# Contiguous 8 KB expert pieces, slot weights in parts, and down pieces by column halves in a one-core mixture-of-experts block

## The reference

```python
h = modulate(rms_norm(x, norm_ffn_g), shift, scale)      # 256 x 1024
scores = sigmoid(h @ router_w)                           # 16 experts, a group of 4 is picked, the top 2 in it
for e in range(16):
    he = silu(h @ w_gate[e]) * (h @ w_up[e])             # 1024 -> 512
    out = out + combine[:, e:e + 1] * (he @ w_down[e])   # 512 -> 1024
x = x + gate_ffn * out
return rms_norm(x, final_norm_g)
```

## Time and profile before

| | us |
|---|---|
| median of three runs | 624.14 |
| the profiled execution | 625.4 |
| its span, first to last instruction | 623.5 |
| TensorE busy | 579.7 (93%) |
| VectorE busy | 316.7 (51%) |
| ScalarE busy | 229.3 (37%) |

### The profile page before, as it was taken

How to read it: one execution, slowest core, us unless ns; L and a number is a source line. 1 busy time by engine, 2 the same in 40 slices (tenths; PEclk the granted TensorE clock), 3 DMA queues, 4 the chain that set the end, 5 groups by cost and what they waited for, 6 DMA issues and landing times.

```text
span 623.5 us, 8315 instructions
## 1 busy us (share of the span) xinstructions
PE 579.7 (93%) x3522; PEld 428.6 (69%) x3522; DVE 316.7 (51%) x467; ACT 229.3 (37%) x312; POOL 5.7 (1%) x14
## 2 busy tenths in 40 slices
PE   1599999999999999999999999989999999999784
PEld 0499988999998888999999885534543533533232
DVE  3797976767569786786464754312202122220203
ACT  4425748444555365376543434201201111110103
POOL 3000000000000000000000000000000000000000
PEclk9799999999999999999999998999999999999997
DMA  8996553785857944744599897399999999999981
GB/s 316 362 387 227 203 203 130 276 290 219 300 216 284 399 155 162 270 139 165 174 387 357 320 383 268 114 398 389 399 387 400 387 402 387 402 387 401 387 350 69
DMA packets 80584, 184.77 MB, mean 296 GB/s; under 512 B 5561, under 2 KB 5665, under 8 KB 78497
## 3 DMA queue, kind: packets, MB, share of 16 engines
q1 hardware_dynamic: 78018, 184.06, 79.6%
q10 hardware_dynamic: 2528, 0.16, 0.3%
HBM read 183.16 MB, written 1.05 MB: 295 GB/s over the span
## 4 chain that ended last, share of the span: by engine, by line
PE 82%; DMA 9%; DVE 4%; ACT 2%; SPq 2%; issue 1%; DVEq 0%; ACTq 0%
PE ps L1357 29%; PE ps L1365 15%; PE ps L1568 15%; PE ps L1580 7%; DMA ring<-in_w_down_e_dram 3%; DMA ring<-in_w_gate_e_dram 2%; DMA ring<-in_w_up_e_dram 2%; DMA raw<-in_w_in_dram 2%; PE ps L1604 2%; PE ps L1556 2%; PE ps L1345 1%; SPq L444 1%; PE ps L1523 1%; PE ps L1434 1%; PE ps L1470 1%
## 5 line engine op out<-in xcount | busy, mean ns | idle before, releaser
L803 DVE TENSOR_TENSOR lo<-raw,hi 128x2048 fp32r<-128x2048 f32 x52 | 118.8, 2291 | 43.3 <-ACT hi L539 43.0
L1357 PE MATMUL ps<-u_hi,hi 128*128 128x256 f32 x432 | 124.4, 288 | 1.1 <-DVE u_lo L869 1.1
L1357 PE MATMUL ps<-u_lo,hi 128*128 128x256 f32 x432 | 122.2, 283 | 0.0
L1357 PE MATMUL ps<-u_hi,lo 128*128 128x256 f32 x432 | 122.2, 283 | 0.0
L1568 PE MATMUL ps<-ring,xe_t 128*64 128x512 f32 x512 | 113.8, 594 | 7.6 <-DMA ring<-in_w_up_e_dram 3.9
L539 ACT CAST hi<-raw 128x2048 fp32r<-128x2048 f32 x52 | 98.7, 1906 | 51.4 <-PE ps L1357 24.6
L1568 PEld LDWEIGHTS ps<-ring,xe_t 128*64 128x64 f32 x512 | 37.5, 137 | 75.3 <-issue 75.2
L1357 PEld LDWEIGHTS ps<-u_hi,hi 128*128 128x128 f32 x432 | 82.8, 192 | 1.5 <-DVE u_lo L869 1.3
L1357 PEld LDWEIGHTS ps<-u_lo,hi 128*128 128x128 f32 x432 | 82.8, 192 | 0.2
L1357 PEld LDWEIGHTS ps<-u_hi,lo 128*128 128x128 f32 x432 | 82.8, 192 | 0.0
L1580 PE MATMUL ps<-ring,he_t 128*64 128x512 f32 x256 | 57.1, 596 | 1.5 <-DMA ring<-in_w_down_e_dram 0.7
(11 more groups left out here) (297 smaller groups left out, 803.3 us busy)
## 6 DMA issues: line engine op xcount, KB each, us to landing
raw<-in_w_in_dram SPq DMA_DIRECT2D x42, 1024.0 KB, 5.0
ring<-in_w_gate_e_dram SPq DMA_DIRECT2D x32, 1024.0 KB, 14.6
ring<-in_w_up_e_dram SPq DMA_DIRECT2D x32, 1024.0 KB, 14.2
ring<-in_w_down_e_dram SPq DMA_DIRECT2D x32, 1024.0 KB, 14.4
raw<-in_ada_w_dram SPq DMA_DIRECT2D x16, 1024.0 KB, 5.0
first_ada<-in_ada_w_dram SPq DMA_DIRECT2D x16, 512.0 KB, 11.6
raw<-in_w_branch_m_dram SPq DMA_DIRECT2D x4, 1024.0 KB, 7.2
raw<-in_w_out_dram SPq DMA_DIRECT2D x4, 1024.0 KB, 6.3
```

What stands on the lines that cost most here:

```text
L803: V.tensor_tensor(lo[b % RING][:], src[:], hi[b % RING][:].bitcast(F32), ALU.subtract).then_inc(lo_ready, 1)
L1357: ins = mm(dst, w[:, k, cols], x[:, k0 + k, :], start=(first and c % 2 == 0 and k == 0 and n == 0), stop=(end and k == KB - 1 and n == 2), ...
```

## The change

Pieces: a piece of w_gate or w_up is now rows h * 512 + 4p + k, k = 0 to 3, in partition p, so that one partition reads 8 KB from one place; a piece of w_down is rows h * 256 + 2p + k, k = 0 and 1, also 8 KB. The other operand must lie in the same order. So x_res is read at a step of four words where it is transposed and where `xg_hi` and `xg_lo` are made (`near`, `nearby`, `dealt`), the router's weights and the norm's gain are loaded in that order, the two rows of `mod` are copied in that order to `mod_p` by ScalarE before TensorE turns them, and `he` is transposed at a step of two words.

Slot weights: VectorE splits them once into high and low fp32r parts (`weights`), the matmul has four columns in place of two and both operands in fp32r, and `w_slot` is the sum of two columns.

Last pieces: the last four pieces (w_down of experts 14 and 15) are loaded by column halves: first all rows of the left 512 columns, in two DMAs an expert, then the right columns, in two DMAs an expert with a semaphore for the second. TensorE finishes the left half (`last_down(0, ...)`) before the right.

End: y's left half is gated, rounded and split after the left half of down, and scattered before the right half is ready; four dummy matmuls follow. The root's table is loaded ahead of the last rounding; the squares of both left halves come before those of the right; the left results are multiplied by the gain on VectorE early and scaled by ScalarE at the end, the right ones are made on VectorE.

```diff
             def load(slot, p, part, e):
                 matrix, half = PARTS[part]
-                w = matrices[matrix][(2 * p + e) % NE].rearrange("(k p) n -> p k n", p=P)
-                k = w.shape[1] // 2
-                sp.dma_start(ring[slot][:].rearrange("p (k n) -> p k n", k=k), w[:, half * k:(half + 1) * k, :]
-                             ).then_inc(ring_loaded[slot], 16)
+                w = matrices[matrix][(2 * p + e) % NE].rearrange("(h p k) n -> p h (k n)", h=2, p=P)
+                sp.dma_start(ring[slot][:], w[:, half, :]).then_inc(ring_loaded[slot], 16)
...
+            def load_columns(slot, e, h, q_of, done):
+
+                w = matrices["down"][NE - 2 + e].rearrange("(h p k) n -> p h k n", h=2, p=P)
+                for q in q_of:
+                    sp.dma_start(ring[slot][:].rearrange("p (k n) -> p k n", k=KB)[:, 2 * q:2 * q + 2, :],
+                                 w[:, q, :, h * NB:(h + 1) * NB]).then_inc(done, 16)
+
+            for e in range(2):
+                n = CHUNKS - 4 + e
+                sp.wait_ge(chunk_used, n - RSLOTS + 1)
+                load_columns(n % RSLOTS, e, 0, (0, 1), ring_loaded[n % RSLOTS])
+            for q in range(2):
+                for e in range(2):
+                    n = CHUNKS - 2 + e
+                    sp.wait_ge(chunk_used, n - RSLOTS + 1)
+                    load_columns(n % RSLOTS, e, 1, (q,), last_loaded[e] if q else ring_loaded[n % RSLOTS])
...
-            act.dma_start(rows[96:104, :], A["norm_ffn_g"][0].rearrange("(c p) -> c p", p=P)).then_inc(rows_loaded, 16)
+            act.dma_start(ffn_g[:], A["norm_ffn_g"][0].rearrange("(h p k) -> p h k", h=2, p=P)).then_inc(rows_loaded, 16)
...
+                if s == M_TURN_AT[1]:
+
+                    after(act, "a_score3")
+                    act.wait_ge(ada_done, ADA_FIRST + ADA_REST)
+                    for m in range(2):
+                        ins = nc.scalar.copy(dealt(mod_p[:, m, :]), nearby(mod[:, 1 + m, :]))
+                    event(ins, "mod_p")
...
-                event(A_(xg_hi[:, t, :], x_res[:, t, :], ACT.Copy, scale=st[:, 14 + t:15 + t]), f"xg_hi{t}")
+                event(A_(dealt(xg_hi[:, t, :]), nearby(x_res[:, t, :]), ACT.Copy, scale=st[:, 14 + t:15 + t]), f"xg_hi{t}")
...
+            def last_norm():
+
+                for n in range(2 * TT):
+                    if n:
+                        act.wait_ge(squared, n)
+                    last_square(n % TT, n // TT)
+                    if n >= TT:
+                        t = n - TT
+                        act.wait_ge(last_var, t + 1)
+                        A_(st[:, 32 + t:33 + t], st[:, 20 + t:21 + t], ACT.Sqrt).then_inc(last_sqrt, 1)
+                for t in range(TT):
+                    act.wait_ge(last_rms, t + 1)
+                    A_(result[:, t, 0:NB], result[:, t, 0:NB], ACT.Copy, scale=st[:, 34 + t:35 + t]).then_inc(out_act, 1)
...
-                V.scalar_tensor_tensor(out=xg_lo[:, t, :], in0=x_res[:, t, :], scalar=st[:, 14 + t:15 + t],
-                                       in1=xg_hi[:, t, :].bitcast(F32), op0=ALU.mult, op1=ALU.subtract).then_inc(xg_split, 1)
+                for h in range(2):
+                    view = (slice(None), t, slice(h * NB, (h + 1) * NB))
+                    ins = V.scalar_tensor_tensor(out=dealt(xg_lo[view]), in0=nearby(x_res[view]), scalar=st[:, 14 + t:15 + t],
+                                                 in1=dealt(xg_hi[view].bitcast(F32)), op0=ALU.mult, op1=ALU.subtract)
+                ins.then_inc(xg_split, 1)
+            split_weights(weights, comb_tab[:, :, 0:NE], 1).then_inc(weights_split, 1)
...
-                    ins = mm(ps[7][:, T:T + 2], onehot[:, t, col:col + 2 * SLOTS].bitcast(F32), weights[:, t, :],
+                    ins = mm(ps[7][:, T:T + 4], onehot[:, t, col:col + 2 * SLOTS], pair[:, t].rearrange("p e w -> p (e w)"),
                              start=(t == 0), stop=(t == TT - 1))
...
-                    ins = tr(ps[6][:, k * P:(k + 1) * P], he[:, k * P:(k + 1) * P], ident[:])
+                    ins = tr(ps[6][:, k * P:(k + 1) * P], he[:, near(0, k, 2)], ident[:])
...
+                    slots = [(2 * (p * NPART + 4) + e) % RSLOTS for e in range(2)]
+                    for e in range(2):
+                        pe.wait_ge(ring_loaded[slots[e]], 16 * ((CHUNKS - 4 + e) // RSLOTS + 2))
+                    last_down(0, range(KB), slots)
+                    slots = group_slots(p * NPART + 5)
+                    last_down(1, (0, 1), slots)
+                    for e in range(2):
+                        pe.wait_ge(last_loaded[e], 16)
+                    last_down(1, (2, 3), slots)
...
+                if h == 0:
+                    for _ in range(4):
+                        mm(ps[4][:], scat[1][:, 0:P], y_hi_e[:, 0:NB], start=True, stop=True)
```

More of the change, by code:

```diff
@@ L109, with near, nearby, dealt @@
 CHUNKS = 2 * PAIRS * 6
+def near(start, kk, k):
+    return slice(start + kk // k * k * P + kk % k, start + (kk // k + 1) * k * P, k)
+def nearby(row):
+    return row.rearrange("q (h p k) -> q h k p", p=P, k=KB)
+def dealt(row):
+    return row.rearrange("q (h k p) -> q h k p", p=P, k=KB)
 PARTS = [(matrix, half) for matrix in ("gate", "up", "down") for half in range(2)]
@@ L189, in build @@
         scat = [at("scat0", 174, [P, T], F32R), at("scat1", 175, [P, T], F32R)]
+        mod_p = at("mod_p", 120, [P, 2, D])
         result = at("result", 120, [P, TT, D])
@@ L315, in plan @@
                 if s == M_TURN_AT[1]:
-                    act.append("ha_hi"); dve.append("ha_lo")
+                    act += ["ha_hi", "mod_p"]; dve.append("ha_lo")
                 if s == FFN_COL_AT[1]:
@@ L775, in _ @@
                 round_y(VISITS * PAIRS - 1)
+                last_norm()
             with act.If(again == 0):
+                A_(st[:, 31:32], st[:, 2:3], ACT.Sqrt)
                 round_y(PAIRS - 1)
[L779 to L789 removed]
+                last_norm()
         @block.vector
@@ L1186, in fill_xe, with gate_y @@
                 ins.then_inc(xe_dve, 1)
-            def gate_y():
-                for h in range(2):
+            def gate_y(halves=(0, 1)):
+                for h in halves:
                     ins = V.tensor_tensor(y_e[:, h * NB:(h + 1) * NB], ps[6 + h][:], mod[:, 3, h * NB:(h + 1) * NB], ALU.mult)
@@ L1203, in take_slots @@
                     rows_s = slice(64 * s, 64 * s + 64)
-                    ins = V.tensor_copy(w_slot[rows_s, side:side + 1], ps[7][rows_s, T + s:T + s + 1])
+                    ins = V.tensor_reduce(w_slot[rows_s, side:side + 1], ps[7][rows_s, T + 2 * s:T + 2 * s + 2], AX_X, ALU.add)
                 ins.then_inc(scat_ready, 1)
@@ L1485, in _ @@
                 if s in FFN_COL_AT:
-                    pe.wait_ge(ada_done, ADA_FIRST + ADA_REST)
-                    after(pe, "a_turned3")
+                    after(pe, "mod_p", "a_turned3")
                     m = FFN_COL_AT.index(s)
                     for k in range(KT):
-                        ins = mm(ps[6][:, KT * m + k:KT * m + k + 1], mod[:, 1 + m, k * P:(k + 1) * P], ones[:, 0:1],
+                        ins = mm(ps[6][:, KT * m + k:KT * m + k + 1], mod_p[:, m, k * P:(k + 1) * P], ones[:, 0:1],
                                  start=True, stop=True)
@@ L1583, in down, with last_down, turn_slots @@
                                 ins.then_inc(chunk_used, 1)
-            def turn_slots(col, weights):
+            def last_down(h, kk_of, slots):
+                for kk in kk_of:
+                    for s in range(2):
+                        w = ring[slots[s]][:].rearrange("p (k n) -> p k n", k=KB)
+                        ins = mm(ps[6 + h][64 * s:64 * s + 64, :], he_t[:, kk, s * SLOTS:(s + 1) * SLOTS], w[:, kk, :],
+                                 start=(kk == 0), stop=(kk == KB - 1))
+                        if kk == KB - 1:
+                            ins.then_inc(chunk_used, 1)
+            def turn_slots(col, pair):
                 for t in range(TT):
@@ L1660, in _ @@
                 pe.wait_ge(he_t_ready, p + 1)
-                for half in range(2):
-                    down(half, group_slots(p * NPART + 4 + half))
+                if p < PAIRS - 1:
+                    for half in range(2):
+                        down(half, group_slots(p * NPART + 4 + half))
+                else:
+                    slots = [(2 * (p * NPART + 4) + e) % RSLOTS for e in range(2)]
[7 more added lines that the diff above has]
+                    last_down(1, (2, 3), slots)
             after(pe, "many")
```

92 lines of the change are left out of this document (48 added, 44 removed).

## The result

The changed kernel took **616.39 us** (median of 5, 615.92 to 619.51) against 624.14 for the kernel before (622.63 to 625.43, 5): a ratio of 0.9885, 95% interval 0.9858 to 0.9913. Forecast were 613.4 and a range of 609.8 to 618.5; against the kernel before that is a gain of 10.7 us forecast and of 7.8 measured. The profiled execution took 615.92 us, of which 614.0 are the span.

A forecast was written before the change was run, and what follows sets the result against it. Late expert weights set the end; without them (-9.5 us) TensorE binds. Last down at 602.8 plus a 9.7 tail gives a 612.5 span, 614.4 for the profiled execution, 613.4 us median; range 609.8 to 618.5 (8 in 10).

The forecast's parts named there:

- The bound and the 8 KB rows: Expert stage: weights come late; 8 KB rows at 416 GB/s end that, -9.5 us, leaving TensorE the bound.
- The rival that memory sets the limit: Expert weight stream: DMAs do not speed up with longer rows, 621.2 us; chance 0.09.
- the one of places that collide: Expert weight stream: engines' reads meet in one part of memory; at 365 GB/s the run takes 637 us; chance 0.05.
- TensorE's path: TensorE's work up to the last down matmul: 601.65 - 1.2 + 1.5 + 0.3 + 0.5 = 602.8 us.
- Slot weights -1.2: Slot-weight matmuls: two fp32r records replace four fp32 ones, -1.2 us over eight pairs (bounds -0.9 to -1.4).
- xg_lo +1.5: VectorE before the second gather: four stepped instructions replace two, +1.5 us (bounds +0.2 to +2.5).
- mod_p +0.3: ScalarE's two copies before TensorE turns mod_p: mostly covered, +0.3 us (0 to 1.5).
- Transposes of x_res +0.5: TensorE's 16 transposes of x_res read at a step of four words: +0.5 us.
- Transposes of he 0: TensorE's transposes of he at a step of two words, eight times four: no cost.
- Rival (b): Stepped reads double he's transposes, eight times 0.49, path +3.9: 617.3 us; chance 0.22 together with (a).
- The tail: From the last down to the end: column halves and reordered end take 9.7 us against 12.4, -2.7 (-2 to -3.3).
- (a): 8 KB rows run at 407, stream stays the bound, xg_lo costs its upper bound: 616.6 us; chance 0.22 with (b).

The follow-up runs named there:

- Experiment 7: Changed kernel with the right half of each token tile stored before the left: 619.23 us.
- experiments 5 and 6: Changed kernel with the last four down pieces whole, tail dummies kept: 621.04 us; changed kernel without the four tail dummies: 619.37 us.
- experiments 6 to 9: Changed kernel, singly: no tail dummies 619.37 us; right half stored first 619.23; dummies before the mod_p wait 619.27; dummies before the x_res transpose waits 619.23.
- changed, 1st and 2nd: The changed kernel with no further edit, measured twice: 616.39 us, then 616.9 us as a yardstick.
- mod_p filled: Changed kernel with four plain fp32 dummy matmuls ahead of TensorE's wait for mod_p: 619.27 us.
- x_res filled: Changed kernel with three dummy matmuls ahead of each of TensorE's two waits for the x_res transposes: 619.23 us.
- all filled: Changed kernel with dummies in TensorE's idle stretches between 310 and 425 us, second tile's start sums moved, right half stored first: 619.24 us.
- filled once: Edits of the all filled kernel, but one dummy at each of three places and eight after xg_hi in place of ten: 614.98 us.
- experiment 2: Changed kernel with ring pieces loaded in 4 KB rows, two DMAs of 512 KB a piece: 622.14 us.

## Why the prediction was right, step by step

**The bound and the 8 KB rows: right.** 421 GB/s against 416 (and 418 by the second way), no wait for the ring, last landing about 597.2 against 596.8, pair periods to 0.1 us. The single ada block of the earlier trace rows was a good witness, and the fixed cost in a row, which I had worked out as 8.4 ns, is 9.2. The rival that memory sets the limit falls, and so does the one of places that collide. The Trainium skill (DMA: Bandwidth & Descriptors, Where 436 GB/s comes from) has the memory side at some 358 GB/s a core and the fabric at 435. The 421 measured here over 130 us, with one core at work, are above the first, so it did not bind here, and below the second.

**TensorE's path: forecast 602.8 for the end of the last down, measured 603.33.** The terms, with what the profile gives for each:
- Slot weights -1.2: -1.8 (0.22 a pair, below the lower bound).
- xg_lo +1.5: +1.8, the mean of four being 1.12 us, where VectorE's adjacent ones take 0.74. (The 3.2 that the prediction set beside its term uses a row of the Trainium skill, Vector Engine (DVE) Microarchitecture Reference, section 5.2, for both sources or the destination stepping. Here one source steps, and 3.2 did not come.)
- mod_p +0.3: +0.9. The two copies took 4.1 us in place of my 3.3; ScalarE pays a step of four words with 2.1 us against 1.05 (the adjacent cast to y_hi, L735, of the same size; least, median and most in ns):
```profile
L723 ACT COPY mod_p<-mod x2: 2099/2122/2144, 312.3 to 314.3; 128x1024 f32<-128x1024 f32 x2
```
```profile
L735 ACT CAST y_hi<-sig_gm x2: 1047/1049/1051, 349.3 to 357.0; 128x1024 fp32r<-128x1024 f32 x2
```
- Transposes of x_res +0.5: some +0.15.
- Transposes of he 0: **+0.8**, 0.1 in each of eight pairs. The prediction counted x_res alone and put he at nothing. The matmuls' records are about as long as before (283 ns against 273); the loads of the stationary operand, which read he, are half as long again:
```profile
L1671 PEld LDWEIGHTS ps<-ident,he x32: 195/209/219, 413.8 to 594.9; 128*128 128x128 f32 x32
L1671 PE MATMUL ps<-ident,he x32: 281/283/388, 413.8 to 595.1; 128*128 128x128 f32 x32
```
The same load in the kernel before:
```profile
L1597 PEld LDWEIGHTS ps<-ident,he x32: 138/140/144, 411.3 to 602.3; 128*128 128x128 f32 x32
```
In pair 2 the second of the four matmuls starts 0.22 us after the first, where it was 0.17, and the others follow at 120 ns in place of 109: together the 0.1. That the load sets this pace is my reading of it and was not tried by itself. The Trainium skill (Advanced Engine Details and Errata, SBUF Cachelines) says that two hits in 16 bytes absorb the latency. The trace does not agree: he has two, and the load takes 209 ns in place of 140. Rival (b) had the direction, at a fifth of its price, and the prediction's sign of being wrong, transposes of he above 0.5 us for four, did come, with 0.60.
- Together these miss by 0.75. The clock gives back 0.2: the fall at 319 cost 1.5 (block 43 took 7.35 us in place of 5.86), and the one that the kernel before has at 381 was absent in this execution (start sums 3.5 in place of 5.2). 0.75 - 0.2 is the 0.5 measured. That the sum came so near is in part luck: five terms missed by 0.3 to 0.8 each, with both signs, and two falls of the clock, which it did not have, cancel.

**The tail: forecast 9.7, measured 10.7.** Up to the last result it took 6.7 us, forecast 6.8. From there I let the end follow after 2.45 us, as before, and a second store issue of 0.4. It followed after 3.95 (610.05 to 614.0), because all four stores queue behind the wait for ScalarE's half. Experiment 7 gives 0.8 of this back. The sum had no order of waits in it; that is the term that was mis-sized, 2.85 for 3.95. The clock in it was right, but not for its reason: the dummies are not what kept it at 1.00 (experiments 5 and 6).

**The median.** The span was 614.0 against 612.5. The other half of the miss is my step from the profiled execution to the median: I took off 1.26 us because that of the kernel before lay above its median, while that of the changed kernel lay 0.47 below its own. (By the text's own numbers that step gives 613.1; I wrote 613.4.) The measured 616.39 lies in the stretch from 615.5 to 620 that the prediction gave to (a) and (b), though neither happened: the rate was 421, and he cost 0.8, not 3.9. The 3.0 us between forecast and median are 1.0 of tail, 0.5 of path and 1.5 of the step from one execution to the median. What goes with the spread of the executions is the granted clock. The changed kernel's are 614.0, 614.1 and 614.4 us at a mean clock of 0.985 and 617.1 and 617.5 at 0.980 and 0.979; 0.006 of 615 us is 3.7 us of full clock, or two falls of 3.4 us at half. The kernel before spreads alike, in the fifteen runs beside experiments 6 to 9 from 620.6 at 0.992 to 625.0 at 0.981.

**What the falls are.** The clock records of the traces (start in us) between 300 and 600 us:

| kernel | wait for mod_p | x_res waits | wait for xg_lo | he waits of pair 0 |
|---|---|---|---|---|
| before | (no wait) | 381.3 | | |
| changed, 1st and 2nd | 319.3; 317.6 (6.8 us) | | | |
| 2 KB; 4 KB rows | 319.7; none | none; 382.0 | | none; 416.1 |
| mod_p on GpSimd | (no wait) | 380.5 (6.8 us) | 397.6 | |
| xg_lo adjacent | 318.1 | 382.9 | | |
| whole last pieces | 318.9 | 383.8 | | |
| no tail dummies | 318.1 | 383.0 | | 417.1 |
| right half first | 318.0 | 382.9 (6.8 us) | 399.9 | 420.4 |
| mod_p filled | (filled) | 384.3 | | 418.4 |
| x_res filled | 318.3 | (filled) | 400.2 | 420.7 |
| all filled | (filled) | (filled) | (filled) | (filled) |
| filled once | 319.1 | (filled) | (filled) | (filled) |

Each fall but those marked lasts 3.4 us, stands at 0.50 (1.2 GHz) and costs up to 1.7. Where the x_res waits stand open, a fall came in 8 of 11 profiles; behind the 1.9 us for xg_lo in 3 of 10, behind the waits for he in 5 of 12. Where they are filled, it came in none of 3, 2 and 2. For x_res that is a clear difference; two profiles at each of the other places would be few. The mean clocks of the runs without a trace bear it out: all six of the filled kernel stand at 0.989 to 0.990, as its profile without a fall does, while the changed kernel's nine executions reach 0.985 at most. That these idle stretches of 0.7 to 1.9 us let the clock fall is shown as far as these counts go; that it is chance in which of them it does is the reading that fits them.

Two things are open. At 319 us it fell in 8 of 9 profiles with the wait open, also with 0.9 us of filler, but in neither of the two with 3.6 us nor of the two without the wait. The 16 one-column matmuls that follow (1.95 us) may have a part together with the wait, but not by themselves, since both profiles without the wait have them too. And filling one place seems to matter for the others: two of ten executions with mod_p filled and three of five with x_res filled reach 0.989 to 0.991, though their other waits stand open. The mean clock alone can't tell a missing fall from a shorter ramp at the start (6.8 us in the profile of experiment 2, 10.2 in all others), so this stays a hint.

The Trainium skill (TensorE: Matmul & The Clock Gate, Part 1) says that one kernel can meet the gate differently from run to run. The trace agrees: two profiles of the changed kernel have the fall at 319.3 us for 3.4 us and at 317.6 for 6.8.

## What to carry to other kernels

Work out the time of a DMA row as a fixed part and a part for its bytes from two row lengths that the kernel already has; here that foretold 313.6 ns for the third, and 311.3 were measured. When a large wait is removed, price the small ones that are left by what they do to TensorE's clock too, and look whether independent work can stand in them (here the start sums, which took a wait from 1.94 to 0.25 us). Count a filler from a row of its own type before it goes in. Behind a reordering of the last stage read the queue that stores the result: an in-order wait for the slower half held a finished half for 1.0 us and cost 0.8.

## What the runs showed of the hardware that I had not expected

- The stationary operand of TensorE pays for a step: loads of 128x128 in fp32 go from 140 to 209 ns at a step of two words, and 212 at four. The four transposes take 0.60 us in place of 0.49.
- ScalarE pays more for a step of four words than VectorE does: 2.1 us for 128x1024 against 1.05 for adjacent ones, twice as long, where VectorE's 128x512 take 1.12 against 0.74.
- The mean granted clock can differ by what four falls of 3.4 us make between executions of one kernel (0.974 and 0.985 in experiment 7), and a spread of 4 us goes with it. The filled kernel spreads by 0.8.
- A 128x512 matmul in plain fp32 costs 0.86 us in two instructions, its fp32r twin 0.23: fillers have to be counted in their own type.
- In both variants with halved DMAs TensorE stood 1.9 and 2.0 us without a releaser before the last scatters, where the changed kernel shows none there. That stays open.
